# Attention in one inference step: probabilities turned in 32x32 blocks on VectorE instead of 128x128 on TensorE

## What is computed

```python
def gqa_block(qb, k, v):                      # 8 heads, 2 key heads, 64 wide
    s = einsum('bqhgd,bshd->bhgqs', qb, k) * HEAD_DIM ** -0.5
    p = softmax(s, axis=-1)
    return einsum('bhgqs,bshd->bqhgd', p, v)

def diff_block(qb, k, v, lam):                # 4 heads, two maps each, values 128 wide
    s = einsum('bqhmd,bshmd->bhmqs', qb, k) * HEAD_DIM ** -0.5
    p = softmax(s, axis=-1)
    a = p[:, :, 0] - lam * p[:, :, 1]
    return einsum('bhqs,bshe->bqhe', a, v)
```

## Time and profile before

| What | Value |
|---|---|
| Median of 3 runs | 1145.94 us (1145.12 to 1146.94) |
| The profiled execution's own time | 1145.81 us |
| Its span, first to last instruction | 1144.0 us |
| PE busy | 1097.6 us, 96% of the span |
| DVE, ACT, POOL busy | 528.1 us (46%), 363.2 us (32%), 132.4 us (12%) |
| Granted PE clock, mean | 0.992 of full speed |
| Attention, first score product to the last tile of the first gate product | 170.6 to 325.8 us |

### The profile page before, as it was taken

The page is one execution under the profiler, slowest core; times in us unless marked ns, Lnnn a source line. Parts: engine busy times, 40 slices in busy tenths (PEclk is TensorE's granted clock), DMA queues, the critical chain, the costliest instruction groups (busy, mean ns, idle before and its releaser), DMA issues.

```text
span 1144.0 us, 28118 instructions
## 1 busy us (share of the span) xinstructions
PE 1097.6 (96%) x12524; PEld 828.2 (72%) x12524; DVE 528.1 (46%) x961; ACT 363.2 (32%) x846; POOL 132.4 (12%) x173
## 2 busy tenths in 40 slices
PE   6999999999999999999998999999999999999993
PEld 4679875666677777777877877777777777777761
DVE  4574538879958142334976033332233223333235
ACT  4333327778753223022163221222222222211103
POOL 2332300000000000002012111111110111110021
PEclk9999999999999999999999999999999999999997
DMA  9932242111031545359987999999999999999993
GB/s 359 299 107 68 77 84 63 35 31 41 1 109 38 184 147 147 106 190 300 355 303 320 402 398 406 407 405 409 414 406 405 408 404 408 405 408 405 410 321 143
DMA packets 86747, 295.32 MB, mean 258 GB/s; under 512 B 27249, under 2 KB 28530, under 8 KB 62050
## 3 DMA queue, kind: packets, MB, share of 16 engines
q1 hardware_dynamic: 79104, 269.77, 61.5%
q0 software_dynamic: 6528, 20.10, 6.1%
q10 hardware_dynamic: 994, 3.65, 0.9%
HBM read 273.25 MB, written 15.00 MB: 252 GB/s over the span
## 4 chain that ended last, share of the span: by engine, by line
PE 85%; DMA 7%; issue 2%; ACT 2%; DVE 2%; SPq 1%; POOLq 0%; POOL 0%; ACTq 0%; DVEq 0%
PE ps L1207 39%; PE ps L772 10%; PE ps L774 9%; PE ps L773 9%; PE ps L994 4%; PE ps L1013 3%; PE ps L1032 2%; PE ps L1036 2%; DMA x_dram<-y_row,rows_t 2%; DMA x_dram<-xn_p 1%; DMA raw_first<-in_w_in_dram 1%; DMA x_f<-x_dram 1%; PE ps L794 1%; DMA raw<-in_w_in_dram 1%; PE ps L978 1%
## 5 line engine op out<-in xcount | busy, mean ns | idle before, releaser
L2124 DVE SCALAR_TENSOR_TENSOR y_row<-ps,gates,gate_q 32x256 f32<-32x256 f32 (+1 forms) x184 | 88.3, 480 | 238.5 <-PE ps L1207 236.0
L1564 ACT ACTIVATE h_t<-ps 128x256 f32<-128x256 f32 x48 | 15.0, 384 | 374.7 <-PE ps L1207 374.7
L772 PE MATMUL ps<-w_hi,ht 128*128 128x512 f32 (+1 forms) x320 | 124.2, 388 | 0.6 <-DVE q_n L1728 0.6
L774 PE MATMUL ps<-w_hi,ht 128*128 128x512 f32 (+1 forms) x320 | 121.8, 381 | 0.0
L773 PE MATMUL ps<-raw_lo,ht 128*128 128x512 f32 (+1 forms) x320 | 121.7, 380 | 0.0
L1207 PE MATMUL ps<-late,xe 128*32 128x256 f32 x1824 | 103.6, 379 | 0.0
L537 DVE TENSOR_TENSOR raw_lo<-raw,w_hi 128x1024 fp32r<-128x1024 f32 x48 | 58.2, 1234 | 78.9 <-ACT w_hi L532 78.2
L1207 PEld LDWEIGHTS ps<-late,xe 128*32 128x32 f32 x1824 | 77.0, 110 | 23.3
L1207 PE MATMUL ps<-raw,xe 128*32 128x256 f32 x1392 | 88.1, 379 | 0.9 <-issue 0.8
L532 ACT ACTIVATE w_hi<-raw 128x1024 fp32r<-128x1024 f32 x48 | 48.7, 1053 | 123.6 <-DMA raw<-in_w_in_dram 68.1
L2354 POOL DMA_INDIRECT xg<-x_dram,rows x48 | 46.1, 961 | 320.7 <-PE ps L1207 293.2
(11 more groups left out here) (315 smaller groups left out, 1831.0 us busy)
## 6 DMA issues: line engine op xcount, KB each, us to landing
late<-in_w_exp_down_dram SPq DMA_DIRECT2D x25, 1024.0 KB, 20.4
late<-in_w_exp_up_dram SPq DMA_DIRECT2D x21, 1024.0 KB, 28.8
late<-in_w_exp_gate_dram SPq DMA_DIRECT2D x17, 1024.0 KB, 24.7
raw<-in_w_in_dram SPq DMA_DIRECT2D x16, 1024.0 KB, 5.5
raw<-in_w_exp_gate_dram SPq DMA_DIRECT2D x16, 1024.0 KB
raw_gate<-in_w_exp_up_dram SPq DMA_DIRECT2D x14, 1024.0 KB
raw<-in_w_exp_up_dram SPq DMA_DIRECT2D x13, 1024.0 KB
raw_gate<-in_w_exp_down_dram SPq DMA_DIRECT2D x13, 1024.0 KB
```

Of the source, the lines that this page charges most:

```text
L772: pe.matmul(b, stat_hi(k, tt), hi[:, kk, :], start=first, stop=False)
L774: mm = pe.matmul(b, stat_lo(k, tt), hi[:, kk, :], start=False, stop=last)
L2124: return dve.scalar_tensor_tensor(y_row[n % 2][32 * v:32 * v + count, 256 * q:256 * q + 256], bank(b, o, o + 256, src), gates[src, n % EG, ...
```

## The change

PE no longer transposes probabilities. DVE's `transpose` turns each 32x32 block of them where it stands. After it a partition no longer holds a query but a key (the one with that number in its block of 32), and the four groups of 32 partitions hold different queries. So `values` works with 32 keys to a product: four products side by side, one for each group of 32 rows, each into a bank of its own (banks 4 to 7). The values must then stand on each group of 32 partitions: SP stores them to DRAM and loads them four times (`v_rep`).

- A pair's values come as three parts of 8 blocks, in the first three slots of the next pair, and 4 blocks of context. A block is 4 products for a differential pair (128 value columns, 128 queries) and 8 for a plain one (64 value columns).
- POOL normalises: two `tensor_scalar` to a slot, and a `tensor_tensor` to subtract in the differential pairs, each on 768 columns of a latent slot. DVE keeps the reciprocals.
- The queries are turned in projections 3 and 4, in ten groups of four transposes each; ACT copies each group, stores it to DRAM, and SP loads each map twice into `q_t`, 64 partitions each.
- ACT makes two copies for a pair's output, and no copies of turned probabilities.
- In projection 4 ACT makes its four `split_hi` one to each half and between the query groups, no longer all four ahead.
- Ten tiles of `ht` are spilled and reloaded, and PE needs them at half 1 of projection 5.

```diff
-LAG = 2
+VALUE_PARTS = 3
+KB, KBL = KEYS // 32, (PAST + LAT) // 32
-SPILLED = 3
+SPILLED = 10
+KEY_GROUPS = [("a", 0, 0), ("b", 0, 0), ("b", 0, 1), ("q", 0, 0), ("q", 1, 0), ("a", 1, 0), ("q", 2, 0), ("a", 2, 0),
+              ("q", 3, 0), ("q", 0, 1), ("a", "ctx", 0), ("q", 4, 0), ("q", 5, 0), ("q", 6, 0), ("q", 7, 0), ("q", 4, 1),
+              ("b", "ctx", 0), ("b", 1, 0), ("b", 1, 1), ("b", 2, 0), ("b", 2, 1)]
+KB_KEYS = {0: [("q", 0, 0), ("q", 1, 0)], 1: [("a", 1, 0), ("q", 2, 0)], 2: [("a", 2, 0), ("q", 3, 0)],
+           3: [("q", 0, 1), ("a", "ctx", 0)]}
+VB_KEYS = {(0, 0): ("q", 4, 0), (0, 3): ("q", 5, 0), (1, 1): ("q", 6, 0), (1, 3): ("q", 7, 0), (2, 0): ("q", 4, 1),
+           (2, 1): ("b", "ctx", 0), (2, 4): ("b", 1, 0), (3, 0): ("b", 1, 1), (3, 1): ("b", 2, 0), (3, 2): ("b", 2, 1)}
...
+                    def load_values(p):
+                        h = 1 + p - PLAIN if p >= PLAIN else 0
+                        if p:
+                            sp.wait_ge(s_vrep, values_loaded(p) - 64)
+                        for a in range(4):
+                            sp.dma_start(v_rep[values_of(p)][32 * a:32 * a + 32, :, :],
+                                         v_dram[:, h, :].rearrange("(b c) n -> c b n", c=32)).then_inc(s_vrep, 16)
...
+                    for p in range(2, PAIRS):
+                        load_query(2 * p)
+                        load_query(2 * p + 1)
+                        if PLAIN < p:
+                            sp.wait_ge(s_pv, p - 1)
+                            load_values(p)
                     sp.wait_ge(s_spill, 16)
-                    sp.wait_ge(s_ptr, len(PIECES))
+                    sp.wait_ge(s_pv, PAIRS - 1)
                     sp.dma_start(ht[:, 0:SPILLED, :].bitcast(F32), ht_dram.bitcast(F32)).then_inc(s_refill, 16)
...
+            def values(p, part):
+                w, pt = v_rep[values_of(p)], p_t[(p + 1) % 2]
+                heads = 2 if p < PLAIN else 1
+                if part == 0:
+                    pe.wait_ge(s_vrep, values_loaded(p))
+                    pe.wait_ge(s_ptr, TURNED[NT * p + NTL - 1])
+                    if p:
+                        pe.wait_ge(s_oev, p)
+                n = KBL // VALUE_PARTS
+                for b in range(part * n, part * n + n):
+                    for a in range(4):
+                        for v in range(heads):
+                            rows, cols = slice(32 * a, 32 * a + 32), slice(P // heads * v, P // heads * (v + 1))
+                            mm = pe.matmul(bank(4 + a, 0, P, cols), w[rows, b, cols], pt[rows, v, :, b, :], start=(b == 0),
+                                           stop=(b == KBL - 1))
...
+            for i in range(len(PUS)):
+                if i < 2:
                     for _ in range(2):
                         pe.matmul(bank(7, 0, KEY_PAIRS * P), q_t[:, 0, 0:P], keys_t[:, 0, :], start=True, stop=True)
                 if i + 1 < len(PUS):
                     scores(2 * i + 2)
                     scores(2 * i + 3)
+                p, t = PUS[i]
+                if p and t < VALUE_PARTS:
+                    values(p - 1, t)
+            pe.wait_ge(s_exp, len(UNITS))
+            pe.wait_ge(s_lo, SPLIT_OF[gemm_half(5, 0)] + 1)
+            first_gates(0, range(NTL))
+            for part in range(VALUE_PARTS):
+                values(PAIRS - 1, part)
...
+                if kind == "q":
+                    g4 = Q_GROUPS.index(group)
+                    act.activation(q_stage[:, g4 % 4, :], bank(6 + n % 2), ACT.Copy).then_inc(s_kev, 1)
+                    act.wait_ge(s_kev, n + 1)
+                    if g4:
+                        act.wait_ge(s_qst, 16 * g4)
...
-            lead(4, end_b + 2)
-            for hh in (2, 3):
+            for hh in range(4):
+                if hh < 3:
+                    split_hi(act, gemm_half(4, hh) + 2)
+                if hh == 2:
+                    split_hi(act, gemm_half(4, 3) + 2)
                 for t in range(NT):
                     if (hh, t) in VB_KEYS:
                         key_copy(VB_KEYS[hh, t])
...
             row_max(0)
             row_max(1)
+            for i in range(len(PUS)):
                 if i + 1 < len(PUS):
                     row_max(2 * i + 2)
+                inverse_sums(i)
+                if i:
+                    turn_probs(2 * i - 2)
+                if i + 1 < len(PUS):
                     row_max(2 * i + 3)
+                if i:
+                    turn_probs(2 * i - 1)
...
+            for i, (p, t) in enumerate(PUS):
+                cols, o = KTL * P if t < NTL else P, 2 * i % 8
+                a, b = prob_row(2 * i)[:, 0:cols], prob_row(2 * i + 1)[:, 0:cols]
+                g = 2 * HB + p - PLAIN
+                pool.wait_ge(s_inv, i + 1)
+                if p < PLAIN:
+                    pool.tensor_scalar(a, a, row_inv[:, o:o + 1], one, ALU.mult, ALU.mult).then_inc(s_nrm, 1)
+                    pool.tensor_scalar(b, b, row_inv[:, o + 1:o + 2], one, ALU.mult, ALU.mult).then_inc(s_second, 1)
+                else:
+                    pool.tensor_scalar(a, a, row_inv[:, o:o + 1], one, ALU.mult, ALU.mult).then_inc(s_nrm, 1)
+                    pool.tensor_scalar(b, b, row_inv[:, o + 1:o + 2], lam[:, g:g + 1], ALU.mult, ALU.mult)\
+                        .then_inc(s_second, 1)
+                    pool.wait_ge(s_nrm, i + 1)
+                    pool.wait_ge(s_second, i + 1)
+                    pool.tensor_tensor(a, a, b, ALU.subtract).then_inc(s_comb, 1)
```

390 lines of the change are left out of this document (136 added, 254 removed).

## The result

The changed kernel takes 1177.03 us in the median of 4 runs (1174.70 to 1179.04), the kernel before 1146.09 (4 runs): a ratio of 1.027, 95% interval 1.0245 to 1.0294. The forecast was 1138, in 1128 to 1160, so it missed in sign and size. The profiled execution took 1175.55 us, its span is 1173.7, to be set against the 1144.0 of the earlier trace rows.

The account below looks back on a forecast made before the run. PE was taken to bound the attention, and a pair's new length to be the longest of four things. From 1145.8 us, pairs -14.6, front +6.0 and tail +1.0 gave 1138.2, so 1138, range 1128 to 1160.

Parts of the forecast that it names:

- The three unknown prices: Attention slots: a DVE turn 0.95 us, a POOL scaling of 768 columns 0.94, a POOL subtraction 1.80.
- My reading of the copies: POOL's prices: the 1700 ns copy began beside DVE's two-input subtraction, so the lower ends (780 ns copy) were taken.
- The price of an instruction of values: PE's values: 27 ns for 128 columns, row groups side by side, so 1.73 us a part, plain or differential.
- The front's parts: Before the first scores: added query groups, a copy wait and a rotation wait, less 1.4 gained; +6.0 us.
- Sum of the pairs: Attention pairs: plain 16.6 us against 20.0, differential 16.7 against 17.0, four of each; 14.6 us gained.
- the ring: Slots with values: waits through maximum, exponent, scores, values and layout changes; two slots last 7.51 us, 3.75 each.
- At a full clock: Attention before the change: PE busy throughout plain pairs of 20.0 us and differential ones of 17.0, its clock full.
- The first, POOL as the bound: Rival, 16 latent differential slots: POOL bounds; with 4.8 us a slot, pairs of 20.8, total 1155; chance 0.22.
- The turn: Rival, DVE in the attention: a turn costs 1.9 us, a plain pair 24.3, total 1169; chance 0.10.
- the row groups: Rival, PE's values: row groups overlap only two deep, 1.75 us more in 21 slots, total 1158; chance 0.12.
- The tail: Last scores to last gate tile: 13.4 us against 12.4, four gate tiles hidden in POOL's time; +1.0.
- The reload: Spilled tiles, two projections before the weights' use: 3200 KB, up to 20 us, 24 available; costed at nothing.

Follow-up runs that it names:

- run 12: Short unread products put where PE waits anyway, on top of run 10: 1156.14 us, ratio 1.0082.
- Run 4: Changed kernel with DVE's reciprocals and next two maxima ahead of the turn that waits for POOL, in differential pairs: 1166.59 us, ratio 1.0173.
- run 5: Changed kernel with a pair's values in seven gaps of PE's list, not three parts, and output copies one slot later: 1167.98 us, ratio 1.0188.
- run 6: Changed kernel with the second branch's values stored and first loaded later, behind the third and fourth pairs' queries: 1176.99 us, ratio 1.0266.
- run 7: Changed kernel with the edits of run 1, Run 4, run 5 and run 6 together: 1160.65 us, ratio 1.0118.
- run 8: run 7 with ACT, not POOL, scaling the first map of a differential pair: 1161.07 us, ratio 1.0126.
- run 9: run 7 with the four loads of a head's second-branch values issued one to a slot, not at once: 1155.97 us, ratio 1.0082.
- run 1: Changed kernel with ACT's four high parts made ahead again in projection 4, not one to each half: 1174.91 us, ratio 1.0245.
- run 3: Changed kernel with POOL's subtraction of the second map left out, so part of the result is missing: 1166.72 us, one run.
- run 10: run 7 with both ACT's scaling of run 8 and the spaced loads of run 9: 1156.73 us, ratio 1.0092.

## Why the prediction was wrong

**What held.** The three unknown prices, within 5%. POOL's additions and scalings did not vary (means of 980, 981 and 1808 ns over 16 each) though a maximum or a turn of DVE ran beside most of them. The Trainium skill, "GPSIMD Engine Reference", Key points, names conflicts over the shared SBUF interfaces with VectorE instructions in a two-port mode or with two SBUF inputs, which agrees. My reading of the copies in the earlier trace rows was wrong all the same, and the low price in part luck: the copy of 780 ns (48.78 to 49.56) ran beside DVE's subtraction (48.90 to 50.64) as the one of 1700 did. The additions of those rows tell it better: 0.79 us twice beside two-input operations of DVE (114.85 and 118.86), 0.46 twice with DVE idle (121.85 and 124.29). The price of an instruction of values was right too: two pieces of 64 and 48 instructions differ by 0.22 us in run 12, 14 ns each for the plain pairs (forecast 13.5); in the differential pairs pieces of 32 and 24 differ by 0.22, 27.5 ns each (forecast 27). What was missing is some 0.3 us of start and end per part, 2.07 where I had 1.73. The front's parts held: 2.62 us of wait for 2.5, 0.67 for the copy of ("q", 0, 1) for 0.7; its miss of 1.7 is the clock.

**The step that failed: "Sum of the pairs".** I made a pair the longest of four sums, one for each engine and one for the ring, each counted slot by slot, and put the context slot at a third of a slot "and 0.3 for its waits". Four things were wrong in it.

- *The order at the border.* I reasoned in the ring that DVE's order sets the second maximum behind the first, but not what the turn in that list waits for in a differential pair, nor that the reciprocal stands behind a maximum of the next slot. In latent slots neither matters, POOL has work. Behind the short slot POOL runs dry twice, 1.72 + 2.84 us of the 21.6. Run 4 shows it by undoing it: 16.5.
- *PE's place for the values.* "PE's list puts the values between" was how I took it; it puts them behind both units' scores, in one piece, and the first piece falls where DVE has only the context slot's short turns to do: a hole of 2.55 us in the fourth pair (run 5 removed it, and left 0.8 to 0.9 at a border).
- *PE's clock.* "At a full clock" was a row of before and I carried it over, though I had taken over 4 us in 20 of work off PE (15.6 us busy at a full clock in the fourth pair of run 5). Its price is 1.2 to 1.3 us in a plain pair at 0.83 to 0.91 (run 12). I had named a clock below full as a sign of a wrong forecast and gave it no rival.
- *PE's instructions.* The page's first line, 28118 against 32044, and the 150 PE instructions of a plain pair against 486 show the growth only afterwards, but I had the count: 64 products of two instructions and as many weight loads in a plain part, where a slot before had 12 transposes and 12 instructions of values. I priced their time on PE and not their way to it: 4.1 us in the second pair and 4.9 in the whole attention, 6.2 to 7.9 in runs 6 to 9.

A fifth, smaller: I counted a gain of 3.4 for each of four plain pairs, but the first, which has no values, took 16.6 before as well.

By place, the second pair is 8.2 us above its forecast, the sixth and seventh 4.2 and 4.9, and the eighth 5.4 above its length before; the third and fourth are only 2.4 and 2.7 above, and shorter than before. By runs 4, 5 and 12 the causes are of the size of the miss in the pairs; how its 31 us divide among them can't be told exactly, since one wait covers another (the gains of runs 4 and 5 add to 19.5, and with runs 1 and 6 the four together gave 16.4).

**Rivals.** The first, POOL as the bound, had half of the place, the differential pairs, and the wrong cause: POOL cost what I said. The turn was not dear, and the row groups do work side by side. The Trainium skill, "TensorE: Matmul & The Clock Gate", section "Wait — 56ns, not 53.3ns?", gives a floor of about 25 ns from start to start; across row groups 14 ns were measured, so it does not hold there.

**The tail** cost 3.0 for the forecast 1.0: the last gate tiles wait 0.98 us for the copy of the last output, and the first four did not hide in POOL's time: they ran from 341.17 at a clock of 0.62, and the values stood behind them until 345.70, 1.4 us after the last turn that they needed (344.34). **The reload** I had costed at nothing. No semaphore waited for it; but in runs 3 to 5, 7 to 10 and 12 PE had "issue" waits of 1.13 to 1.93 us in the last pair's values, while it was under way or shortly after; that it caused them is not shown.

No version beat the kernel before. In run 12 it is 143.7 us from the start of the first scores to the end of the last, before 144.0: the mended pairs, with their waits for instructions, pay just for themselves. Lost on top are 3.4 us in the front (first scores at 173.9 for 170.5), 3.9 from the end of the last scores to the first product of the head means, and some 3 behind it that no run explains.

## What to carry to other kernels

Don't sum a stage by engines and slots alone: at the shortest slot of a loop, follow each engine's list in order and ask of each wait what stands behind it, for there the work that covers a wait is missing. When work is taken off PE, ask whether its clock stays up without it, and price the clock from rows at both levels. And when few long instructions become many short ones, count them against the time in which a block of instructions arrives, and look at what the DMA engines carry meanwhile.
